# One product and one sum of 4096 columns per slot of cached keys, in place of two of 2048

## The reference

```
k_past = cache_k[page_table].reshape(n_seq, past, N_HEADS, 2, HEAD_DIM)
v_past = cache_v[page_table].reshape(n_seq, past, N_HEADS, V_DIM)
...
s_past = jnp.einsum('bqhcd,bshcd->bhcqs', q, k_past, preferred_element_type=jnp.float32) * scale
s_new = jnp.einsum('bqhcd,bshcd->bhcqs', q, k_new, preferred_element_type=jnp.float32) * scale
...
w = diff_combine(jnp.concatenate([s_past, s_new], axis=-1), lam).astype(v_new.dtype)
return (jnp.einsum('bhqs,bshe->bqhe', w[..., :P], v_past)
        + jnp.einsum('bhqs,bshe->bqhe', w[..., P:], v_new))
```

## Time and profile before

| | |
|---|---|
| median of 3 runs | 1354.79 us (1353.63 to 1358.72) |
| the profiled execution | 1357.79 us |
| its span (first to last instruction) | 1356.0 us |
| PE, DVE, ACT busy, share of the span | 87%, 61%, 41% |
| mean granted TensorE clock | 0.906 of full speed |
| first score product starts, last sum of scores starts | 619.1, 854.5 us |

### The profile page before, as it was taken

How to read it: one execution, slowest core, us unless ns; L and a number is a source line. 1 busy time by engine, 2 the same in 40 slices (tenths; PEclk the granted TensorE clock), 3 DMA queues, 4 the chain that set the end, 5 groups by cost and what they waited for, 6 DMA issues and landing times.

```text
span 1356.0 us, 19558 instructions
## 1 busy us (share of the span) xinstructions
PE 1173.1 (87%) x7298; PEld 964.9 (71%) x7298; DVE 828.1 (61%) x1046; ACT 558.9 (41%) x685; POOL 25.8 (2%) x31
## 2 busy tenths in 40 slices
PE   3797878899999999889968557678779999999975
PEld 1595747788888888778844344366568888888874
DVE  1436376656656563677768989544856566565455
ACT  1332235655555551454221221242455555555321
POOL 2000001000000000000000000000010000000000
PEclk9898988999999999899866777778789999999988
DMA  9939451899999978663779999937249999999400
GB/s 331 387 112 365 144 188 50 302 334 338 336 340 332 337 279 294 231 230 125 260 279 338 355 339 340 352 133 250 84 138 351 329 337 334 341 337 336 161 2 32
DMA packets 143713, 355.40 MB, mean 262 GB/s; under 512 B 4706, under 2 KB 4899, under 8 KB 143652
## 3 DMA queue, kind: packets, MB, share of 16 engines
q1 hardware_dynamic: 142388, 350.98, 72.4%
q0 software_dynamic: 1264, 3.59, 0.8%
HBM read 351.28 MB, written 3.28 MB: 261 GB/s over the span
## 4 chain that ended last, share of the span: by engine, by line
PE 69%; DVE 17%; DMA 4%; SPq 4%; ACT 3%; issue 2%; ACTq 0%; DVEq 0%
PE gu L652 26%; PE pj L671 17%; PE pj L412 13%; DVE reg L2020 3%; DVE wring L2017 3%; PE gu L481 3%; PE tb L446 2%; PE pj L514 2%; PE tb L443 2%; DMA wring<-in_ada_w 2%; DMA wring<-in_a_w_in 1%; PE pj L873 1%; SPq L992 1%; ACT whi L1342 1%; DVE wlo L1617 1%
## 5 line engine op out<-in xcount | busy, mean ns | idle before, releaser
L1849 DVE TENSOR_TENSOR wlo<-wring,whi 128x2048 fp32r<-128x2048 f32 x128 | 290.1, 2289 | 103.8 <-ACT whi L1342 103.7
L1342 ACT ACTIVATE whi<-wring 128x2048 fp32r<-128x2048 f32 x128 | 244.7, 1916 | 144.6 <-PE gu L652 144.6
L671 PEld LDWEIGHTS pj<-tokB,wring 128*128 128x128 f32 x2048 | 233.4, 192 | 3.4 <-issue 0.7
L671 PE MATMUL pj<-tokB,wring 128*128 128x128 f32 x2048 | 234.0, 275 | 0.0
L652 PE MATMUL gu<-whi,xhi 128*128 128x512 f32 x512 | 207.6, 405 | 12.2 <-DVE xlo L1877 12.2
L652 PE MATMUL gu<-wlo,xhi 128*128 128x512 f32 x512 | 204.5, 399 | 0.0
L652 PE MATMUL gu<-whi,xlo 128*128 128x512 f32 x512 | 204.2, 399 | 0.0
L1231 ACT ACTIVATE reg<-pj 128x264 f32<-128x264 f32 (+2 forms) x149 | 73.8, 498 | 300.3 <-PE pj L671 145.1
L652 PEld LDWEIGHTS gu<-whi,xhi 128*128 128x128 f32 x512 | 98.0, 191 | 34.6 <-DVE xlo L1877 6.6
L652 PEld LDWEIGHTS gu<-whi,xlo 128*128 128x128 f32 x512 | 97.9, 191 | 23.4
L652 PEld LDWEIGHTS gu<-wlo,xhi 128*128 128x128 f32 x512 | 98.0, 191 | 21.7
(11 more groups left out here) (338 smaller groups left out, 1773.5 us busy)
## 6 DMA issues: line engine op xcount, KB each, us to landing
wring<-in_moe_w_gate SPq DMA_DIRECT2D x32, 2048.0 KB, 9.5
wring<-in_moe_w_up SPq DMA_DIRECT2D x32, 2048.0 KB, 10.2
wring<-in_moe_w_down SPq DMA_DIRECT2D x32, 2048.0 KB, 9.2
wring<-in_ada_w SPq DMA_DIRECT2D x24, 2048.0 KB, 14.1
wring<-in_cache_k SPq DMA_DIRECT2D x64, 512.0 KB, 4.9
wring<-in_cache_v SPq DMA_DIRECT2D x64, 512.0 KB, 5.2
wring<-in_a_w_in SPq DMA_DIRECT2D x4, 2048.0 KB, 20.0
wring<-in_a_w_out SPq DMA_DIRECT2D x2, 2048.0 KB, 17.2
```

Of the source, the lines that this page charges most:

```text
L671: m = pe.matmul(bank[:, i * P:(i + 1) * P], w[:, k, f * P:(f + 1) * P], aT[:, k, :], start=(k == 0), stop=(k == FB - 1))
L1342: act.activation(whi[q], quarter(wring, q, s), ACT.Copy).then_inc(hi_ready, 1)
L1849: dve.tensor_tensor(quarter(wlo, q, s), quarter(wring, q, s), whi[q].bitcast(F32), ALU.subtract).then_inc(lo_ready, 1)
```

## The change

The two halves of a slot are joined. `scores(s, k)` multiplies all four pages of a slot at once and sums 4096 columns to 64. A sample so has two score calls, 4 instructions. The small steps of a turn keep their order among themselves, but they now stand in two places only: `rope`, `key_max` and `key_exp` between the two calls, and all of `row_max`, `key_sum`, `key_weights`, `row_factors`, `largest` behind the second. In the part before the loop two `tile_split` calls now stand next to each other. Nothing else is changed: PE, ACT, SP and POOL have the same programs, and the arithmetic is the same.

```diff
--- before.py
+++ after.py
@@ -2004,23 +2004,18 @@
                 dve.tensor_tensor(q, q, bank[:, 0, :], ALU.add)
                 empty(dve.tensor_tensor(k, k, bank[:, 1, :], ALU.add))
 
-            def scores(s, k, q):
+            def scores(s, k):
 
                 slot, count = cache_slot("k", s, k)
-                if q == 0:
-                    if k == 0:
-
-                        dve.wait_ge(pj_evac, at[f"spread{s}"])
-                    dve.wait_ge(slot_in[slot], at["cache_loads"][slot] + 16 * count)
-
-                keys = wring[:, slot, q * 2 * D:(q + 1) * 2 * D]
-                link(dve.tensor_tensor(keys.rearrange("p (g n) -> p g n", g=2), keys.rearrange("p (g n) -> p g n", g=2),
-                                       qbc[:, s % 2:s % 2 + 1, :].to_broadcast([P, 2, D]), ALU.mult))
-                g0 = 4 * k + 2 * q
-                i = dve.tensor_reduce(sS[:, s, g0:g0 + 2, :].rearrange("p g x -> p (g x)").unsqueeze(2),
-                                      keys.rearrange("p (x d) -> p x d", d=HD), AX.X, ALU.add)
-                if q == 1:
-                    i.then_inc(keys_used, 1)
+                if k == 0:
+
+                    dve.wait_ge(pj_evac, at[f"spread{s}"])
+                dve.wait_ge(slot_in[slot], at["cache_loads"][slot] + 16 * count)
+
+                keys = wring[:, slot, :].rearrange("p (g n) -> p g n", g=4)
+                link(dve.tensor_tensor(keys, keys, qbc[:, s % 2:s % 2 + 1, :].to_broadcast([P, 4, D]), ALU.mult))
+                dve.tensor_reduce(sS[:, s, 4 * k:4 * k + 4, :].rearrange("p g x -> p (g x)").unsqueeze(2),
+                                  wring[:, slot, :].rearrange("p (x d) -> p x d", d=HD), AX.X, ALU.add).then_inc(keys_used, 1)
 
             def largest(s):
 
@@ -2071,13 +2066,11 @@
                 dve.tensor_scalar(pst[:, :, 5:6], pst[:, :, 5:6], nlam[:, 0:1], None, ALU.mult).then_inc(inv_ready, 1)
 
             tile_split()
-            scores(0, 0, 0)
+            scores(0, 0)
             tile_split()
-            scores(0, 0, 1)
             tile_split()
-            scores(0, 1, 0)
+            scores(0, 1)
             tile_split()
-            scores(0, 1, 1)
             rope_sample(uT[:, :, TP:T])
             ready(dve.tensor_tensor(rs[:, 0:64].rearrange("p (h b) -> p h b", b=NB), cqT[:, :, TP:T], uT[:, :, TP:T], ALU.mult))
             tile_split()
@@ -2091,7 +2084,7 @@
             for s in range(1, NB + 2):
                 m = s - 1
                 if s < NB:
-                    scores(s, 0, 0)
+                    scores(s, 0)
                 if s == 1:
                     mod_rows(1, 5)
                 if s <= NB:
@@ -2099,20 +2092,16 @@
                     key_max()
                 if s == 1:
                     tile_split()
-                if s < NB:
-                    scores(s, 0, 1)
                 if s <= NB:
                     key_exp(m)
                 if s < NB:
-                    scores(s, 1, 0)
+                    scores(s, 1)
                 if s <= NB:
                     row_max(m)
                 if s == 1:
                     mod_rows(1, 6)
                 if s <= NB:
                     key_sum(m)
-                if s < NB:
-                    scores(s, 1, 1)
                 if s <= NB:
                     key_weights(m)
                     row_factors(m)
```

## The result

The changed kernel takes 1359.84 us (median of 20 runs, 1355.67 to 1362.57) against 1357.44 us of the kernel before in its 20 runs. The ratio is 1.0020, with a 95% interval of 1.0012 to 1.0028: 2.4 us slower, between 1.6 and 3.8. The profiled execution has a span of 1360.8 us, the one of before 1356.0.

A forecast was written before the change was run, and what follows sets the result against it. DVE's order was taken to bound turns 3 to 7, with DMA close behind. Per turn -0.62 + 1.32 = +0.70 us, +3.5 over five, took the median from 1354.79 to 1358.3 us; range 1352.3 to 1362.6, 88%.

The forecast's parts named there:

- The saving: DVE score calls: joined products and sums of about 4.40 us save 0.31 us a slot, 0.62 a turn.
- The two waits: DVE waits for PE's answers before `key_exp` (0.62 to 0.80 us added) and `key_weights` (0.52 to 0.70) each turn.
- Nothing below 1.14: Floor in us a turn for both added DVE waits, as PE cannot start before DVE ends and DVE works in order.
- The sum on the turns: Turns 3 to 7: -0.62 + 1.32 = +0.70 us each, +3.5 us for five (+2.6 to +7.8).
- the least to be told from no change: Whole kernel's time: about 0.5%, 6.8 us, is what a measurement can tell from no change.
- The part before the loop: PE stands about 1.8 us for the late fourth `tile_split`, covered by 2.12 us of idle time before the `ada_w` tile; costs nothing.
- 0.3 us to spare: Before the loop: what remains of PE's 2.12 us idle time for the `ada_w` load after the 1.8 us delay.
- rival 2: Slower: PE's delay or lower clock before the loop reaches the load chain, up to 6.6 us past the spare, 1364.9; chance 7%.
- The cover of the other steps: In the turns, `row_factors` and ring slots come in time, PE is free; sample 3's keys still wait for loads; priced at nothing.
- The faster rival: Turns 3 to 7: waits cost nothing and saved constant parts stay, about -2.5 us, 1352.3; chance 8%.
- The pages, its other limit: Page loads at 23.85 us a turn hold back some of a 3.1 us gain in turns 4 and 5.
- The end of the attention: What follows the attention depends on its end and moves with it.

The follow-up runs named there:

- order_only: The changed kernel's order, but each score call does two halves of 2048 columns back to back; 1365.17 us against 1356.21 for the kernel before, ratio 1.0066.
- sum_hidden: The changed kernel with `key_sum` moved ahead of `row_max`; 1355.68 us against 1356.21 for the kernel before, ratio 0.9999.
- both_hidden: The changed kernel with `rope` and `key_max` ahead of the first score call from turn 2, `key_sum` ahead of `row_max`; 1354.88 us against 1356.98 before.
- late_exp: The changed kernel with `key_exp` behind the second score call and `largest` between `key_sum` and `key_weights`; 1356.20 us against 1356.22 for the kernel before.
- prelude_only: The kernel before with only sample 0's scores, ahead of the loop, joined; 1356.48 us against 1356.21 for the kernel before, ratio 1.0003.
- loop_only: The changed kernel with sample 0's scores, ahead of the loop, in halves as before; 1359.70 us against 1356.98 for the kernel before, ratio 1.0017.

## Why the prediction was right, point by point

**The saving.** Worked out as 0.62 us a turn from products of 4.40 us; the products take 4.42 us, and `order_only` against the changed kernel gives 0.55 us a turn. The extrapolation was 0.02 us an instruction short, and with four of them in a turn that is the whole difference. One of its two rows was no product: the 1226 ns of the earlier trace rows belong to a subtraction that writes another type. The joined instruction is cheaper than the two: a product of 4096 columns takes 4421 ns where two of 2048 take 4568 (2 x 2284), 147 ns less, and a sum 4420 where two take 4572, 152 ns less. The kernel does not gain by it, since the joined instruction takes the cover from two waits.

**The two waits.** Forecast as 1.14 to 1.50 us a turn over the old spacing, taken as 1.32. Measured in the turn shown: 0.97 - 0.21 = 0.76 for `key_exp` and 0.91 - 0.39 = 0.52 for `key_weights`, 1.28 together. Over the five turns of `order_only`, which have no saving, it is 6.59 / 5 = 1.32. "Nothing below 1.14" was wrong: in turn 6 both products are short and it is (0.76 - 0.21) + (0.91 - 0.39) = 1.07, since PE starts `key_max_rows` 0.05 us after DVE and DVE goes on 0.05 us after PE, where I had put 0.06 and 0.10. That both waits, and nothing else in the turn, are the cost is shown by taking them away: one gone in `sum_hidden`, 2 us less on the turns; both gone in turn 7 of `both_hidden`, 23.91 us; and both gone but for a small rest in turns 6 and 7 of `late_exp`, 24.0.

**The sum on the turns.** Forecast +0.70 a turn and +3.5 us; measured 3.84 / 5 = 0.77 and +3.84 in the profile. The median moved by 2.4 us, with an interval of 1.6 to 3.8 that also holds the forecast 3.5; why it moved by 1.1 us less than the sum is not shown, and the one profiled pair differs by more, 4.8. Both figures lie far under the 6.8 us that I had called the least to be told from no change: 20 runs of each tell 2.4. The time itself, 1359.84, lies 1.5 us over the 1358.3 that I named, because the base moved: the median of before is 1357.44 over 20 runs, and 1354.79 was that of three. That it still lies in the range owes something to the range's width; what bears the sum out are the turns.

**The part before the loop.** PE's stand was forecast as 1.8 us and is 1.71. That it costs nothing was right for a partly different reason. I had 0.3 us to spare; the lower clock behind the stand (0.75 in the window above) used that up and more, as rival 2 describes it: PE starts the `ada_w` tile 18.76 us after the one before, not 17.51. What pays most of it back is that tile, 1.92 us at a granted clock of 1.00 without idle time before it, where it took 2.66 at 0.69. `prelude_only` shows no loss that can be measured.

**The cover of the other steps.** `row_factors` does not wait, PE is free at both places, and the keys of sample 3 still set the start of turn 3. That PE is free at `key_max_rows` cuts both ways: it has been idle there, and it does this product or the prompt scores behind it at the lower clock. In turn 4 the two take 7.17 us at a granted clock of 0.50 (769.03 to 776.20), and before they took 4.08 us at 1.00 (762.05 to 766.13). One thing I passed over: the second `values` of a turn stand behind them on PE, and so the value slots come back later. These matmuls in turn 4, before and after:

```profile
766.13 1.93 PE L873 MATMUL pj<-wring,reg 128*32 128x512 f32 x16
```

```profile
776.21 2.86 PE L873 MATMUL pj<-wring,reg 128*32 128x512 f32 x16
```

They end 13.0 us into the turn before and 21.2 us into it after (turns from 755.10 and 757.86). SP's key loads now wait for them (these rows answer to the earlier trace rows; the issue of eight pages took 10.80 there):

```profile
746.90 12.72 SPq L1120 DMA_DIRECT2D wring<-in_cache_k  x8
...
772.68 11.49 SPq L1120 DMA_DIRECT2D wring<-in_cache_k  x8
...
797.19 12.90 SPq L1120 DMA_DIRECT2D wring<-in_cache_k  x8
```

12.72, 11.49 and 12.90 us. From 735 to 860 us SP waits 11.6 us in all for that work, against 1.6 before and 1.8 in `both_hidden`, where `rope` and `key_max` open the turn. In the changed kernel this costs nothing: its turns are longer than the loads need, and DVE waits for no keys in turns 4 to 7. In `late_exp` it is the bound at the start of turn 5.

**The faster rival.** It would have needed the waits to cost nothing. Hiding them gave the 0.5 us a turn where nothing else came up (turn 7 of `both_hidden`). The pages, its other limit, held DVE back by 0.39 us in `sum_hidden` and by 0.45 and 0.42 in `late_exp`, about where I had put the loads' limit.

**The end of the attention.** The forecast moved it as it was. In the profile it is 0.95 us shorter (first the kernel before, then the changed one):

```profile
858.96 0.37 PE L443 MATMUL tb<-kst,lamx 128*16 128x128 f32 x1 [4.28 <-DVE lamx L2028]
859.93 2.93 PE L851 MATMUL gu<-ws,yT 128*128 128x128 f32 x12 [0.60 <-ACT ws L1473]
```

```profile
864.74 0.27 PE L443 MATMUL tb<-kst,lamx 128*16 128x128 f32 x1 [1.43 <-DVE lamx L2023]
865.71 1.88 PE L851 MATMUL gu<-ws,yT 128*128 128x128 f32 x12 [0.70 <-ACT ws L1473]
```

The weights of a head (second row) take 1.88 us here, at a granted clock of 0.82 and behind short idle times of 1.43 and 0.70 us; in the kernel before they took 2.93 us at 0.50, and PE had been idle for longer, 4.28 us, ahead of the first row's product. Over the kernels run the stretch of turns 8 and 9 scatters by more than 4 us, so I don't count it to the change. Whether the shorter idle time before it is a lasting gain was not tried.

## What to carry to other kernels

Before joining two instructions of an engine that, like DVE in every turn here, runs its program in order, look at what stands between them: if the small steps there ask another engine something, the second half was the cover for the answer, and one way there and back (0.5 to 0.8 us here) costs more than the constant part of an instruction (0.15 us here, 2 x 2284 - 4421 ns). Count the saved constant parts and the uncovered ways in the same turn, and swap the small steps so that one covers the other; a step that moves needs cover itself, as `rope` did. When an engine's turn is close to what its loads need, a slot that comes back later can be the next bound, as in turn 5 of `late_exp`, where DVE waited 0.42 us for keys.

## What the runs showed of the hardware that was not expected

Before the loop PE ran slower behind its longer waits for the load, and standing for one thing could pay for another: the same `ada_w` tile took 1.92 us at a granted clock of 1.00 when PE came to it without idle time (the changed kernel, `prelude_only`), and 2.66 us at 0.69 and 3.64 us at 0.50 after it had stood 2.1 and 2.4 us for the load (before, `loop_only`); behind 0.98 us of idle time it still took 1.92 us at 1.00 (`late_exp`). The two-matmul products took 0.39 to 0.61 us in the same places of different turns: about 0.40 where the granted clock was 1.00 (755.15, 780.37, 794.26 in the changed kernel) and 0.60 where it was 0.50 (743.81, 769.03, 805.38). That is the whole difference between the waits of 0.48 and of 0.70 us before `key_exp`. So a change on DVE alone made PE's answer slower (0.60 us for 0.39 in turn 4), where the question came to PE after 3.15 us of idle time; idle time alone does not settle it, since the product at 794.26 ran at 1.00 behind 3.82 us of it.
